# The split of a weight block ahead of the last product's addition, in the feed-forward part of an encoder layer

## The reference

```python
z = rms_norm(x) @ w_in                        # pool | q | k | v
x = x + rms_norm(concat(pool, attention) @ w_out)
x = x + rms_norm((silu(h @ w_gate) * (h @ w_up)) @ w_down)   # h = rms_norm(x), 2816 channels inside
x = x + (p @ w_ple_proj) * sigmoid(x @ w_ple_gate + b_ple_gate)
```

## Time and profile before

| | us |
|---|---|
| median of 3 runs | 2377.54 (2376.04 to 2378.93) |
| the profiled execution's own time | 2377.34 |
| its span | 2375.3 |
| TensorE busy | 2308.0 (97%) |
| VectorE busy | 1680.4 (71%) |
| ScalarE busy | 1035.9 (44%) |
| GpSimd busy | 957.4 (40%) |

### The profile page before, as it was taken

How to read it: one execution, slowest core, us unless ns; L and a number is a source line. 1 busy time by engine, 2 the same in 40 slices (tenths; PEclk the granted TensorE clock), 3 DMA queues, 4 the chain that set the end, 5 groups by cost and what they waited for, 6 DMA issues and landing times.

```text
span 2375.3 us, 29644 instructions
## 1 busy us (share of the span) xinstructions
PE 2308.0 (97%) x10928; PEld 1909.8 (80%) x10928; DVE 1680.4 (71%) x1753; ACT 1035.9 (44%) x1538; POOL 957.4 (40%) x557
## 2 busy tenths in 40 slices
PE   8999999999989989999999999899999999999999
PEld 6888788888768868888887888788788888877877
DVE  5766788888745688676766555888888865575842
ACT  4433688888734453333333222444343333233221
POOL 0000345545424565354443466444456634550300
PEclk9999999999989999999999999999999999999999
DMA  5223223222448874444537767564557587676431
GB/s 188 82 71 98 85 61 74 61 54 52 71 143 232 251 243 161 150 164 133 173 121 273 296 252 280 164 205 162 169 188 262 202 327 264 249 244 235 159 109 74
DMA packets 337374, 402.75 MB, mean 170 GB/s; under 512 B 36688, under 2 KB 240336, under 8 KB 337104
## 3 DMA queue, kind: packets, MB, share of 16 engines
q1 hardware_dynamic: 337232, 400.87, 51.3%
HBM read 259.18 MB, written 137.43 MB: 167 GB/s over the span
## 4 chain that ended last, share of the span: by engine, by line
PE 84%; DVE 7%; issue 3%; DMA 2%; ACT 2%; SPq 1%; POOL 1%; DVEq 0%; ACTq 0%; POOLq 0%
PE ps L1418 47%; PE ps L1210 31%; PE ps L1213 6%; DVE ring L2160 1%; DVE reg L2168 1%; DMA xb<-x_turned 1%; DMA f_turned<-ev 1%; DVE negmax L2064 1%; DVE pt L2106 0%; DVE fhi L2280 0%; SPq L636 0%; DVE fb L2474 0%; POOL fb L1204 0%; ACT pt L1520 0%; DMA scales<-row_scales 0%
## 5 line engine op out<-in xcount | busy, mean ns | idle before, releaser
L1418 PE MATMUL ps<-reg,ring 128*128 128x512 f32 x5544 | 1272.5, 392 | 20.6 <-DVE ring L2160 14.3
L1418 PEld LDWEIGHTS ps<-reg,ring 128*128 128x128 f32 x5544 | 1047.2, 189 | 244.7 <-DVE ring L2160 18.1
L1520 ACT ACTIVATE ring<-wraw 128x1024 fp32r<-128x1024 f32 (+2 forms) x152 | 143.6, 946 | 399.3 <-PE ps L1418 399.3
L2160 DVE TENSOR_TENSOR ring<-wraw,ring 128x1024 fp32r<-128x1024 f32 (+2 forms) x152 | 227.9, 1500 | 62.5 <-ACT ring L1520 61.8
L1210 PE MATMUL ps<-win,ht 128*128 128x512 f32 (+1 forms) x1152 | 227.7, 358 | 11.1 <-DVE win L2000 10.9
L1210 PEld LDWEIGHTS ps<-win,ht 128*128 128x128 f32 x1152 | 190.8, 191 | 41.8 <-issue 11.5
L1520 ACT ACTIVATE ring<-ws 128x1024 fp32r<-128x1024 f32 (+2 forms) x114 | 108.0, 947 | 247.1 <-PE ps L1418 236.8
L2106 DVE TENSOR_TENSOR pt<-ps,pt 128x512 fp32r<-128x512 f32 x256 | 174.0, 686 | 39.9 <-ACT pt L1520 37.2
L2160 DVE TENSOR_TENSOR ring<-ws,ring 128x1024 fp32r<-128x1024 f32 (+2 forms) x114 | 171.5, 1505 | 42.1 <-ACT ring L1520 41.5
L1210 PE MATMUL ps<-wout,ct 128*128 128x512 f32 x768 | 185.0, 400 | 11.6 <-DVE wout L2087 6.6
L1210 PEld LDWEIGHTS ps<-wout,ct 128*128 128x128 f32 x768 | 144.5, 192 | 43.3 <-DVE wout L2087 7.3
(11 more groups left out here) (204 smaller groups left out, 2924.6 us busy)
## 6 DMA issues: line engine op xcount, KB each, us to landing
reg<-ff_forms SPq DMA_DIRECT2D x42, 1536.0 KB, 10.1
ff_forms<-fhi SPq DMA_DIRECT2D x88, 512.0 KB, 3.2
wraw<-in_w_gate SPq DMA_DIRECT2D x88, 256.0 KB, 4.2
wraw<-in_w_up SPq DMA_DIRECT2D x88, 256.0 KB, 4.6
ff_forms<-ev SPq DMA_DIRECT2D x44, 512.0 KB, 2.9
wraw<-in_w_down SPq DMA_DIRECT2D x48, 384.0 KB, 5.4
reg<-ff_forms SPq DMA_DIRECT2D x14, 1024.0 KB, 6.9
xt_a<-in_xt SPq DMA_DIRECT2D x16, 512.0 KB, 4.4
```

Of the source, the lines that this page charges most:

```text
L1418: last = nc.tensor.matmul(ps[:, 2 * chain + m, :], ring[:, st % 3, a, m, k * P:(k + 1) * P], reg[:, k, i, e, :], start=OPENS[i] and k == 0 ...
L1520: copy = lambda out, src, **k: nc.scalar.activation(out, src, ACT.Copy, **k)
L2160: V.tensor_tensor(ring_block(u, st, 1), weight_source(u, i), f(ring_block(u, st, 0)), ALU.subtract).then_inc(S["w_split"], 1)
```

## The change

In every step of the feed-forward part the split for `st + 2` now comes first in the streams of ScalarE and VectorE. On VectorE it moves ahead of all six additions. On ScalarE it moves ahead of `middle`, which is there at step 2 alone. No instruction is added or removed, and no wait is altered.

```diff
@@ ScalarE @@
             for st in range(NST + 1):
                 u, i = UNITS[min(max(st, 0) // NP, NU - 1)], st % NP
                 inside = 0 <= st < NST
+                if 2 <= st < NST - 2:
+                    weights_hi(st + 2)
                 if inside and i == 2:
                     middle(u)
-                if 2 <= st < NST - 2:
-                    weights_hi(st + 2)
                 if st and i == 0:
@@ VectorE @@
                 before = UNITS[st // NP - 1] if st > 0 and i == 0 else None
+                if 2 <= st < NST - 2:
+                    weights_lo(st + 2)
                 if before:
                     c21_end(before)
                 if inside and i == 2:
                     g_tile(u)
                 if inside and i == 3:
                     c22_middle(u)
                 if inside and i == 4:
                     c22_end(u)
                 if inside and i == 5 and u.down and u.part:
                     c11_end(u)
                 if inside and i == 6:
                     c12_end(u)
-                if 2 <= st < NST - 2:
-                    weights_lo(st + 2)
                 if before and not before.down:
                     gated(before, 3)
```

## The result

The changed kernel takes 2387.73 us (median of 6 runs, 2385.13 to 2390.52), the kernel before 2375.93 in the same comparison: ratio 1.0045, 95% interval 1.0035 to 1.0055, or 8 to 13 us slower. The forecast was 6.1 us more, a time of 2383.6. The page of the changed kernel counts three instructions more than the earlier trace rows; they are semaphore instructions of VectorE's sequencer, and the count of each engine's work is the same.

What follows compares the result with a forecast made beforehand. TensorE, busy 97% of 2375.3 us, was taken as the bound, leaving only its idle stretches and granted clock. Terms -1.4 + 3.7 + 5.0 - 1.2 = +6.1 us on 2377.54 gave 2383.6; own range 2376 to 2389, overall 2370 to 2389.

Steps and rivals of the forecast that it cites:

- signs of being right: Additions 1.15 us into each split; stalls over 2 and 3 us at token sums and root, half clock behind; 1514 stall gone.
- signs of being wrong: Root's wait still under 1.5 us, or no half clock behind it, or stalls inside the regular steps.
- The regular step: Steps between seams: split starts as now, addition ends 2.3 us after the product, covered by later products; cost nothing.
- (a): Gate to down, first sequence, product at 1293.44: split no longer behind `middle` and an addition; 1.4 us gained, bounds 0 to 4.7.
- (b): Second sequence's first fill, product at 1514.41: TensorE gains 3.7 us there, but only as a longer wait at (c).
- (c): Token sums of the norm, unit 23, step 3: TensorE waits longer for step 2's addition; +3.7 us, bounds +0.95 to +5.1.
- slower still: Units 20 to 22: step 4's addition waits with the split behind a square awaiting a load; 2388 to 2391 us; chance 0.10.
- (d): Norm's root on ScalarE, behind the SiLU: stall 0.86 to 3.7 us, plus half clock; +5.0 us, bounds +2.3 to +6.0.
- the estimate by the page: At (d), the split would wait out a whole GpSimd instruction, 1.30 us; the sum would be +7.0 instead of +6.1.
- (e): End of the part, last units: first split no longer behind the store; -1.2 us, bounds -3.9 to +1.7.
- No change: Rival: the terms stand, but the two longer stalls cost no clock; +1.7 us, 2379.2; chance 0.25.
- Faster: Rival: waits for the split go at seams 1293, 1514 and 2118, chain's lag taken up; -13.2 us, 2364.3; chance 0.15.

## Why the prediction held, and where it was off

What was named as the signs of being right is there; so is, in part, one of the signs of being wrong, stalls inside steps (units 21 and 22).

**The regular step** costs nothing, as forecast: units 1 to 9 take 342.72 us in both profiles, although every addition there stands behind its split. In unit 10 of the changed kernel, beside the earlier trace rows:

```profile
1264.31 1.88 DVE L2160 TENSOR_TENSOR ring<-wraw,ring 128x1024 fp32r<-128x1024 f32 x1 [2.81 <-ACT ring L1520]
1266.12 1.21 DVE L2205 TENSOR_TENSOR ev<-ev,ps 128x1024 f32<-128x1024 f32 x1
```

Here the split was stretched to 1.88 us, so the addition ends 4.2 us after its product (which ended at 1263.12), and not 2.3; the product that needs it starts 6.5 us later still.

**(a)** Forecast: a stall of about 1.9 us that `middle` ends, 1.4 us gained. Measured: stalls of 0.78 and 1.65, the second ended by `middle`; the product starts at 1293.07, as forecast, but 0.3 of its 0.4 us were there at unit 10 already. Then 858 matmuls take 195.03 us where 197.61 stood: 2.6 us, because no half clock followed. That size was in part chance: of two repeats of the kernel before, one has full clock after the same stall, one half. Behind a stall of 1.6 to 1.7 us none of five profiles with the changed order there has half clock. With the chain's two additions first, the stall is 1.04.

**(b), (c)** The lead that (b) gives is lost by (c), as forecast. Swapping the additions of steps 3 to 5 was to move nothing, yet the stall at 1497, now ended by the addition of step 5, is 3.78 where 3.03 stood; why is open. The token sums start 1.3 us later than before, after a stall of 4.98 (forecast 6), and the half clock costs 17.94 - 16.50 = 1.4 (forecast 2.2). The 1.3 is not the 1.5 of (c): in the sum (a)'s gain stands beside it, so 0.1 was forecast. What makes it, on VectorE, before and then changed, to be laid beside the earlier trace rows:

```profile
1668.94 3.41 DVE L2280 TENSOR_TENSOR fhi<-ev,fhi 128x1024 fp32r<-128x1024 f32 x1
```
```profile
1669.38 3.40 DVE L2280 TENSOR_TENSOR fhi<-ev,fhi 128x1024 fp32r<-128x1024 f32 x1
...
1673.76 1.22 DVE L2160 TENSOR_TENSOR ring<-wraw,ring 128x1024 fp32r<-128x1024 f32 x1
1674.90 1.21 DVE L2181 TENSOR_TENSOR ev<-ev,ps 128x1024 f32<-128x1024 f32 x1
```

The first row of each is the end of the chain. From its end to the addition of step 2 it was 1.26 us and is 2.12, for the split ahead: 0.86, forecast 0.95. That term was right. The chain's was not. Its last row is only 0.44 us later (forecast 0.5), but TensorE had ended the row at 1293 2.95 us earlier. Counted from that row's end, the chain's last row starts 176.9 to 177.9 us on in the three profiles of the kernel before and 181.3 and 179.8 in the two of the changed one: 2 to 4.4 us late, not 0.5. With the additions of steps 6 and 0 ahead of the split it is 177.9, with these two alone behind it 178.2, with all six behind it and ScalarE as before 180.8: neither set of additions makes the lateness alone. That fits the "slower still" rival, which had a chance of 0.10: the margin of step 4 is lost where the chain, and with it the load, is late. No run moves step 4 alone, so how much is that rival's stays open. In unit 22 of the changed kernel, VectorE waits for a copy behind the square, and the addition goes last:

```profile
1645.42 2.45 DVE L2160 TENSOR_TENSOR ring<-wraw,ring 128x1024 fp32r<-128x1024 f32 x1 [5.11 <-ACT ring L1520]
1647.80 1.21 DVE L2205 TENSOR_TENSOR ev<-ev,ps 128x1024 f32<-128x1024 f32 x1
```

Its product starts at 1649.15, 1.59 us late. The direct price was 0.4 and 1.6 us in units 21 and 22 (in the repeat 1.3 in unit 22 alone), and (c) took it in, as that rival said of its first part.

**(d)** Right in mechanism and size: SiLU starts 4.0 us after the product's end, where it was 1.3, the root's stall 3.56 (forecast 3.7). At 408.33 / 1800 a matmul, 1812 take 411.05; they took 412.97, so half clock cost up to 1.9 (forecast 2.2). The split in front took 1.64, 0.42 over its 1.22 alone; I had put 0.45. It started, at 1701.98, while a GpSimd instruction of 1.30 us had 0.56 to run, and the next one took 2.15:

```profile
1701.24 1.30 POOL L1126 TENSOR_TENSOR ev<-ev,g 128x512 f32<-128x512 f32 x1
...
1702.62 2.15 POOL L1129 TENSOR_TENSOR ev<-ev 128x512 f32<-128x512 f32 x1
```

The Trainium skill, "SBUF — State Buffer", section "SBUF: two separate sides", has each lock the other out for a whole instruction. The rows agree with that within 0.2 us; the estimate by the page was too large because the split met an instruction that was more than half done, not its start.

**(e)** Forecast 1.2 us gained, measured 0.4 (from the start of unit 35 to the last matmul 76.8 us before, 76.4 now), which is nothing beside the scatter: the repeats have 75.6 and 77.2 before, 76.7 changed. The first stalls shrink as said, but the last product now waits 3.10 us for its addition and then runs 12 matmuls in 5.46 us, at half clock.

**The sum.** TensorE leaves the part 2153.95 - 2146.88 = 7.1 us later than in the profile the sum was made against (forecast 6.1). That this is so near is in part luck. Counted from unit 10, (c) came out at 4.2 us and 1.4 of half clock instead of 1.5 and 2.2, its chain being the term that was too small; (a) gave 2.6 instead of 1.4, and (d) cost 0.4 less than forecast, which hid most of it, while (e) gave 0.8 less. The runs differ by more, 10.7 by the ratio, and here the sum's base failed: one profiled execution that was slow in one stretch and quick in another. Behind the part, for which the sum has no term, the two first profiles differ by another 3.5 us. Over the profiles, the part takes 1297.5 us before in the mean and 1306.7 changed, 9.2 more; the stage after it 225.6 and 227.3, so the mean would add up to 10.9. Five profiles can't give this an interval. The measured 2387.73 us lies nearer to the 2388 of "slower still" than to 2383.6, and part of that rival's mechanism is in the lines of unit 22. "No change" is refuted: its condition was that the long stalls cost no clock. "Faster" named the point where it decides, that the root's row stays put; it went from 1703.03 to 1708.62.

## What to carry to other kernels

A list of what TensorE waits for names the last of several inputs; before an input is moved forward, look up who else waits for the work that it passes, above all a chain that goes through several engines and comes back to TensorE at a fixed place. Order is worth choosing by step: here split first, with ScalarE's part, costs nothing that can be told at the steps whose addition has two products' time, and 9 us ((1.0045 - 1.0007) x 2376) more when the two steps that feed such a chain are in it. Moving a consumer of the late value (token sums one step on, the root ahead of the SiLU) gave back about 6 us each.

## What the runs showed of the hardware that was not expected

The clock's answer to a stall is not a function of its length. The 2.8 us at 1293 were followed by 16 matmuls in 6.40 us in two executions and by 28 in a third of the same kernel. The root's stall of 3.56 us in the changed kernel was followed by 10 matmuls in 3.71 us; one of 3.55 in the run with steps 6 and 0 alone was followed by 16, at full clock:

```profile
1710.49:1714.19 3.70, 3.70 (x16) 1.00 0.65 242
```

A single profile can thus be 2.8 us off at one stall, as much as a term of this sum.
